# VectorE in the gated recurrence: the step's updates of q, decay and scores put ahead of the weight's lower half and the modulation's sums

## The reference, cut to what matters

```
mod = silu(cvec) @ ada_w + ada_b                  # the modulation, 6 x 1024 columns
proj = h @ w_in                                   # q, ff, fb, iv, g, hy
k_f = -expm1(logf_f);  k_b = -expm1(logf_b)
S_t = diag(f_t) S_{t-1} + k_t v_t^T               # forward and backward
o_t = S_t^T q_t
o = o_f + o_b;  o = rmsnorm(o) * silu(g)
hyc = dwconv3(hy)                                 # beside it: v, x1, x2 of the long convolution
```

## Time and profile before

| | us |
|---|---|
| median of 3 runs | 908.77 |
| lowest and highest run | 907.77, 908.89 |
| the profiled execution | 908.05 |
| its span, first to last instruction | 906.2 |
| TensorE busy | 887.7 |
| VectorE busy | 714.4 |
| ScalarE busy | 446.7 |

### The profile page before, as it was taken

The page is one execution under the profiler, slowest core; times in us unless marked ns, Lnnn a source line. Parts: engine busy times, 40 slices in busy tenths (PEclk is TensorE's granted clock), DMA queues, the critical chain, the costliest instruction groups (busy, mean ns, idle before and its releaser), DMA issues.

```text
span 906.2 us, 14128 instructions
## 1 busy us (share of the span) xinstructions
PE 887.7 (98%) x5384; PEld 788.9 (87%) x5384; DVE 714.4 (79%) x903; ACT 446.7 (49%) x718; POOL 38.7 (4%) x58
## 2 busy tenths in 40 slices
PE   7999999999999999999999999999999999999997
PEld 4469898998898898778889999999999999998885
DVE  5744764975966985599878899999999999988645
ACT  5835424324334333333566746565565656565443
POOL 2200000100000000101000000000000000000000
PEclk9999999999999999999999999999999999999999
DMA  8765143254044154323801233324313332345703
GB/s 282 261 195 197 60 151 121 50 163 142 28 163 146 45 184 162 94 70 59 244 1 47 76 131 103 109 95 131 99 64 133 116 107 81 131 164 194 261 0 117
DMA packets 39275, 112.76 MB, mean 124 GB/s; under 512 B 4471, under 2 KB 12663, under 8 KB 38568
## 3 DMA queue, kind: packets, MB, share of 16 engines
q1 hardware_dynamic: 33944, 93.58, 30.8%
q0 software_dynamic: 4800, 17.99, 6.6%
q10 hardware_dynamic: 464, 0.30, 0.1%
HBM read 101.48 MB, written 10.37 MB: 123 GB/s over the span
## 4 chain that ended last, share of the span: by engine, by line
PE 88%; DVE 5%; ACT 3%; DMA 2%; issue 2%; ACTq 0%; DVEq 0%; SPq 0%; POOLq 0%
PE ps L2042 19%; PE ps L2043 19%; PE ps L2044 19%; PE ps L2545 14%; PE ps L2263 3%; PE ps L2062 2%; PE ps L2123 2%; PE ps L2400 2%; PE ps L2445 1%; PE ps L2275 1%; DMA part<-in_rates 1%; DMA w<-in_hy_w 1%; PE ps L2070 1%; PE ps L2283 1%; DMA raw<-in_slots 1%
## 5 line engine op out<-in xcount | busy, mean ns | idle before, releaser
L2042 PE MATMUL ps<-h_hi,w_hi 128*128 128x320 f32 x588 | 186.3, 317 | 0.7 <-issue 0.7
L2044 PE MATMUL ps<-h_hi,w_lo 128*128 128x320 f32 x588 | 181.7, 309 | 0.0
L2043 PE MATMUL ps<-h_lo,w_hi 128*128 128x320 f32 x588 | 181.6, 309 | 0.0
L2042 PEld LDWEIGHTS ps<-h_hi,w_hi 128*128 128x128 f32 x588 | 110.7, 188 | 1.4 <-issue 1.4
L2043 PEld LDWEIGHTS ps<-h_lo,w_hi 128*128 128x128 f32 x588 | 110.6, 188 | 0.0
L2044 PEld LDWEIGHTS ps<-h_hi,w_lo 128*128 128x128 f32 x588 | 110.4, 188 | 0.0
L1905 DVE TENSOR_TENSOR w_lo<-raw,w_hi 128x1024 fp32r<-128x1024 f32 (+1 forms) x53 | 64.2, 1213 | 18.6 <-ACT w_hi L1253 17.6
L1253 ACT ACTIVATE w_hi<-raw 128x1024 fp32r<-128x1024 f32 (+1 forms) x53 | 55.5, 1048 | 31.1 <-PE ps L2044 31.0
L1411 DVE TENSOR_TENSOR w_lo<-raw,w_hi 128x1024 fp32r<-128x1024 f32 x42 | 51.1, 1225 | 6.8 <-ACT w_hi L917 5.8
L2042 PE MATMUL ps<-w_hi,h_hi 128*128 128x512 f32 x120 | 49.2, 410 | 0.3 <-issue 0.2
L1905 DVE TENSOR_TENSOR w_lo<-wsum,w_hi 128x1024 fp32r<-128x1024 f32 x38 | 46.4, 1222 | 1.0 <-ACT w_hi L1253 0.4
(11 more groups left out here) (341 smaller groups left out, 2120.5 us busy)
## 6 DMA issues: line engine op xcount, KB each, us to landing
raw<-in_slots SPq DMA_DIRECT2D x138, 512.0 KB, 4.8
acts<-actf POOLq DMA_DIRECT2D x22, 320.0 KB, 2.5
raw<-in_slots SPq DMA_DIRECT2D x24, 256.0 KB, 6.1
xf<-acts SPq DMA_DIRECT2D x12, 320.0 KB, 7.4
wsum<-acts SPq DMA_DIRECT2D x10, 320.0 KB, 7.8
xin<-in_x_sample SPq DMA_DIRECT2D x4, 512.0 KB, 11.3
grow<-gates POOLq DMA_DIRECT2D x2, 1024.0 KB, 11.5
x<-in_x_sample POOLq DMA_DIRECT2D x2, 1024.0 KB, 10.3
```

The source lines that it names most:

```text
L2042: mm(out, lhs[0], rhs[0], start=first, stop=False)
L2043: mm(out, lhs[0], rhs[1], start=False, stop=False)
L2044: return mm(out, lhs[1], rhs[0], start=False, stop=last)
```

## The change

In VectorE's loop over `n`, the wait for the half and `bound_gates`, and then the recurrence's `step`, are moved ahead of `split_lo` and of `sum_groups` (with `make_gain`). `pass_k` stays first and `start_head` last. No instruction is added or taken away, no other engine's order is changed. `split_lo` is called only at even `n`, and `bound_gates` only at odd `n` on tiles that have no sums, so among themselves these two don't change places.

```
@@ -1661,6 +1661,11 @@
                 kind, i = TILES[n // 2]
                 if step_at(n):
                     pass_k(*step_at(n))
+                if n % 2 and kind in ("ff", "fb"):
+                    eng.wait_ge(sem("half_free"), n + 1)
+                    bound_gates(i, int(kind == "fb"))
+                if step_at(n):
+                    step(*step_at(n))
                 for unit in ahead(n):
                     split_lo(unit)
                 if n in ADA_SUM:
@@ -1668,11 +1673,6 @@
                     sum_groups(e)
                     if ADA_ORDER[e] == FINE[1]:
                         make_gain(1, "norm2")
-                if n % 2 and kind in ("ff", "fb"):
-                    eng.wait_ge(sem("half_free"), n + 1)
-                    bound_gates(i, int(kind == "fb"))
-                if step_at(n):
-                    step(*step_at(n))
                 if n % 2 and kind == "fb":
                     start_head(i)
                 if n == 2 * HEAD_TILES - 1:
```

More of the change, by code:

```diff
@@ L1670, in _ @@
                         make_gain(1, "norm2")
[L1671 to L1675, removed]
                 if n % 2 and kind == "fb":
```

## The result

| | before | changed |
|---|---|---|
| median of 5 runs, us | 908.74 | 921.45 |
| lowest and highest | 907.77, 908.89 | 920.81, 927.78 |
| the profiled execution | 908.05 | 920.99 |
| its span | 906.2 | 919.2 |
| mean granted clock | 0.999 | 0.995 |

The changed kernel is slower: the ratio is 1.0158, 95% interval 1.0128 to 1.0188. The forecast was +8.8 us, 917.5, with a range up to 921.5; the medians are 12.7 us apart. The direction and the places were right, the size was not: the median of the changed kernel stands at the very top of the range, and the ratio times the median of before (about 923) lies above it.

A forecast was written before the change was run, and what follows sets the result against it. TensorE was taken to bound the kernel, busy 887.7 of 906.2 us. Late transposes in heads 1, 2, 3 and 0 add 2.4 + 3.2 + 3.1 + 0.1 = 8.8 us to 908.77, giving 917.5, range 913.0 to 921.5.

The forecast's parts named there:

- What bounds, and where: TensorE bounds; its gaps are waits before step 2 (0.89, 1.10, 0.89 us) and 0.61 us at a transpose.
- Part 1: At n = 16, 28, 40, q's update ahead of half and sums: net 0.42 us earlier, step 2's wait about 0.5.
- Part 2, the late slot: At n = 18, 30, 42, 6, later lower halves delay urgent 512 KB transfers and TensorE's transposes: 8.8 us in all.
- L: Landing time of the urgent 512 KB transfer ahead of each head's transpose, taken as 4.2 us.
- no clock to be won: In heads 1 to 3 TensorE's granted clock is 1.00, so only 4 us of gaps can be had.
- each delay stays to the end: Behind each late transpose the steps follow TensorE, so its delay is kept: 2.4, 3.2, 3.1 and 0.1 us.
- Part 3, what costs nothing: The other late halves, the sums and GpSimd's gate stores are covered, at no cost; nearest is n = 16's piece.
- The short landings: Rival: urgent transfers land in 3.2 us each time, adding 5.7 us, for 914.5; chance 0.25.
- the long ones: Rival: urgent transfers share the engines in bursts and land in 5.1 us each time, for 921.1; chance 0.2.
- The kept gain: Rival: rounds don't wait for the transfers, so q's earlier update remains: 907.0, or 905.3; chance 0.04.

The follow-up runs named there:

- kernels 1: Against the kernel before, only in rounds n = 6, 18, 30 and 42 the lower half goes behind the step; 915.50 us, ratio 1.0093.
- kernel 8: Kernel 7 with GpSimd's two gate stores held until TensorE's step 5 of head 1 is done; 904.19 us, ratio 0.9964.
- kernel 2: Against the kernel before, only in rounds n = 14, 26, 38 and 50 the lower half goes behind the step (behind `finish_head`); 912.61 us, ratio 1.0062.
- Kernel 6: The changed kernel with 15, 9 and 15 small matmuls on TensorE ahead of the transposes of n = 20, 32 and 44; 918.05 us, ratio 1.0115.
- kernel 9: The changed kernel with GpSimd's two gate stores held until TensorE's step 5 of head 1 is done; 921.49 us, ratio 1.0149.
- kernel 4: Against the kernel before, only in rounds n = 16, 28 and 40 the lower half and the sums go behind the step; 911.09 us, ratio 1.0036.
- kernel 7: Against the kernel before: lower half behind the step in rounds 16, 28, 40; convolution of 17, 29, 41 one round later, behind its step; 908.44 us, ratio 1.0008.
- kernel 3: Against the kernel before, the whole change except that in rounds n = 6, 18, 30, 42 the lower half stays ahead; 914.33 us, ratio 1.0077.
- Kernel 5: Kernel 4 with GpSimd's two gate stores held until TensorE's step 5 of head 1, which holds head 0's state store too; 907.50 us, ratio 0.9996.

## Why the prediction was right or wrong

*What bounds, and where.* Right. The waits before step 2 and the chain through the raw slot were the places, and kernels 1 and 8 show both.

*Part 1.* Right. q came 0.3 to 0.55 us earlier for a forecast 0.4 to 0.6, VectorE's stretch grew by 1.2 us through `finish_head` for a forecast 1.14 (kernel 2), and TensorE's lead was gone at the transpose. The 0.25 us that head 2 lost again before step 4 wasn't in the sum.

*Part 2, the late slot.* Right as a mechanism, and nearly in size: 10.0 us measured for 8.8. The issue was forecast at 184.75 and came at 185.71, of which 0.8 us is the lateness brought along from head 0. The landings of heads 1 to 3 had a mean of 4.15 for the 4.2 assumed. Head 0 was the one mis-sized: L was 5.16 and not 4.2, 1.15 us for 0.1. That the sum came so near was partly luck, since head 2 was 0.9 us under its term: its transfer landed in 3.21, and its transpose waited 2.46 us, not 3 to 4.

*The step that failed* is the sentence that there was "no clock to be won", and behind it "each delay stays to the end": I priced a wait of TensorE by its length. Behind two of the long ones the granted clock went to its lower level for about 3 us, which cost 1.59 and 1.56 us. Kernel 6 gives it back while the transposes of n = 20 and 44 still wait for their transfers. With it, 10.0 + 3.15 = 13.2; a forecast with every wait right and no term for the clock would have said 919. The spread belongs here too: the changed kernel's five runs lie between 920.81 (mean clock 0.995) and 927.78 (0.987), and before's within 1.1 us.

*Part 3, what costs nothing.* Right for the changed kernel: no wait at a quad or at a half. But the cover of the gate stores was argued too shortly. They were called "far from being needed", which they are; what I left out is that they themselves are in the way. In the changed kernel they were nearly through when the urgent transfer was issued (kernel 9). In kernels 4 and 7 they weren't, and with the state store behind them cost about 3.5 and 4 us; kernel 3 has no twin without them.

*The rivals.* The short landings came true in head 2 alone (3.21), the long ones in head 0. One reading behind them was wrong: before, head 2's transfer (issued at 248.28) had not two but four others behind it within 1.8 us, so its burst was as full as head 1's, and it took 3.2 us all the same. Of the prices, the Trainium skill's fit ("DMA: Bandwidth & Descriptors", the anatomy of one DMA), 3.2 us by an estimate, holds for one of four. The kept gain didn't happen. Kernel 5 shows that q's earlier update alone gives nothing, since step 4 waits instead, and kernel 8 that it takes the convolution and the stores out of the way first.

## What to carry to other kernels

Before an instruction is moved back because its result isn't needed soon, look at what its end releases: here making a weight's lower half freed a buffer, and the transfer into it was on the chain one round later. A wait of TensorE can cost more than its length, because the clock can fall behind it: here the long ones had up to 1.6 us on top, which filling them with small matmuls gave back. And a shorter wait at one step isn't a gain while the engine that ends it has no slack up to the next: here the lower half, the convolution and the stores had to be moved together to get 0.4%.

## What the runs showed of the hardware that was not expected

**The fall of the clock.** In the 2.1 to 2.5 us waits it came in some (2.15, 2.27, 2.31 and 2.44 us) and not in others (2.11, 2.32, 2.46); behind 2.8, 3.0, 3.7, 3.8 and 3.9 us it came each time. Where it came it cost 1.3 to 1.6 us on top of the wait. Its start lay anywhere from 0.4 us before TensorE's first matmul behind the wait (239.59 for 239.97 in kernel 2, 189.21 for 189.59 in kernel 4) to 1.2 us after it (332.56 for 331.32 in the changed kernel).

The Trainium skill ("TensorE: Matmul & The Clock Gate", sections "Part 1: The HAM clock gate" and "HAM oscillation") has a gate with these two levels, and says that matmuls start again at the lower one where each block waits for its transfer. The windows of the changed kernel agree (0.53 behind the wait of n = 20), and kernel 6 shows the other side, 1.00 with the same transfer waited for. Which waits make it fall is taken from the runs alone.

**Stores from GpSimd hold large loads back.** With two 4 KB stores of single elements from GpSimd in flight, and a 128 KB store behind them, 512 KB loads on SyncE's queue took 7.05 us (kernel 4), 6.82 (kernel 3), 7.6 and 11.0 (kernel 7); the loads in their places took 4.7 us in kernel 5, and 4.6 and 3.1 in kernel 8, with the stores moved away. In kernel 4 next to nothing had moved for 2 to 3 us after the load's issue. It takes more than the last of a store: in the changed kernel the second gate store landed 1.35 us after the issue of the urgent load, which took 4.56. In no run are the gate stores delayed and the state store left where it was. That they and not the state store do it is argued from the state stores of heads 1 and 2, which land in 2.2 us with loads of 4.0 us right behind them (212.53 and 214.03 before).

**Left open.** Why the first transfer of a burst takes 3.2 to 3.3 us in head 2 in every kernel and 4.3 to 5.2 in most of the others isn't settled; the gate stores aren't it (4.73 in kernel 5), nor the number of requests right behind it, which before was four in head 1 and four in head 2. What decides about the clock between 2.1 and 2.5 us isn't either. A sixth raw slot, which would take the urgent transfer off the lower half altogether, was not tried.
